# Hybrid-attention block on one core: value products of two heads on the two column halves, turned reciprocals, and three edits in the feed-forward part

## What is computed

```python
h = rms_norm(x, g_pre_mix) * (1.0 + sc1) + sh1
proj = h @ w_in            # 1220 columns: queries, keys, values, latents, indexer
# A: 8 heads, keys of the last 128 positions, a learned sink per head, ALiBi
# B: 8 heads, one shared key/value head; an indexer scores all visible keys,
#    each query keeps its 256 best; softmax over those, ALiBi
mix = concatenate([out_a, out_b]) @ w_o
x = x + gt1 * rms_norm(mix, g_post_mix)
h2 = rms_norm(x, g_pre_ffn) * (1.0 + sc2) + sh2
gate, up = split(h2 @ w_gate_up)
x = x + gt2 * rms_norm((silu(gate) * up) @ w_down, g_post_ffn)
```

## Time and profile before

| what | us |
|---|---|
| median of 3 runs | 3282.39 (3280.31 to 3283.53) |
| profiled execution, its own time | 3280.21 |
| its span, first to last instruction | 3278.4 |
| PE busy | 2893.9 (88%) |
| DVE busy | 1689.7 (52%) |
| ACT busy | 1569.7 (48%) |
| mean granted TensorE clock | 0.929 |

### The profile page before, as it was taken

The page is one execution under the profiler, slowest core; times in us unless marked ns, Lnnn a source line. Parts: engine busy times, 40 slices in busy tenths (PEclk is TensorE's granted clock), DMA queues, the critical chain, the costliest instruction groups (busy, mean ns, idle before and its releaser), DMA issues. The chain is left out here.

```text
span 3278.4 us, 42244 instructions
## 1 busy us (share of the span) xinstructions
PE 2893.9 (88%) x14392; PEld 2338.0 (71%) x14392; DVE 1689.7 (52%) x3088; ACT 1569.7 (48%) x3006; POOL 315.7 (10%) x989
## 2 busy tenths in 40 slices
PE   6678888787887888789898999999999999999997
PEld 2456666666676667678786887888877887888876
DVE  2246768586878868834454443254424443254422
ACT  0457787778777786875333222232223222232222
POOL 0112222212121120120111000000000000000000
PEclk8788888898988888889998999999999999999999
DMA  5000000000000010211465333343334333343323
GB/s 209 8 22 14 23 14 17 11 13 13 14 4 14 14 55 4 110 55 62 138 179 179 95 97 90 122 142 96 97 121 135 102 96 90 122 142 96 99 88 108
DMA packets 286884, 254.86 MB, mean 78 GB/s; under 512 B 8685, under 2 KB 238617, under 8 KB 286617
## 3 DMA queue, kind: packets, MB, share of 16 engines
q1 hardware_dynamic: 282584, 236.32, 23.3%
q10 hardware_dynamic: 4160, 16.78, 1.3%
HBM read 219.50 MB, written 33.57 MB: 77 GB/s over the span
## 5 line engine op out<-in xcount | busy, mean ns | idle before, releaser
L2002 ACT ACTIVATE p_hi<-raw 128x1024 fp32r<-128x1024 f32 x264 | 279.4, 1058 | 691.3 <-PE dbank L1972 352.4
L2079 DVE TENSOR_TENSOR p_lo<-raw,p_hi 128x1024 fp32r<-128x1024 f32 x264 | 323.4, 1225 | 429.6 <-ACT p_hi L2002 429.6
L1322 DVE TENSOR_SCALAR_CACHE_REDUCE above<-score,cand 128x384 uint8<-128x384 f32 (+6 forms) x224 | 315.8, 1410 | 4.3
L1172 ACT ACTIVATE signs<-score,pick 128x512 int8<-128x512 f32 (+6 forms) x224 | 304.4, 1359 | 28.1 <-POOL pick L684 19.7
L1150 ACT ACTIVATE logit<-tbank 128x512 f32<-128x512 f32 (+3 forms) x448 | 214.2, 487 | 209.0 <-PE tbank L903 205.8
L903 PE MATMUL tbank<-ident,logit 128*128 128x128 f32 x1336 | 249.5, 300 | 65.9 <-ACT logit L1140 57.0
L919 PE MATMUL obank<-vb,logit 128*128 128x64 f32 x2176 | 298.5, 282 | 0.0
L1970 PE MATMUL dbank<-p_hi,a_hi 128*128 128x512 f32 x704 | 277.8, 395 | 17.0 <-DVE a_lo L2106 13.8
L919 PEld LDWEIGHTS obank<-vb,logit 128*128 128x128 f32 x2176 | 292.1, 207 | 0.0
L1953 PE MATMUL gbank<-x_hi,p_hi 128*128 128x512 f32 x704 | 275.8, 392 | 14.8 <-DVE p_lo L2079 14.8
L788 PE MATMUL work<-w_in,h_T 128*128 128x512 f32 (+1 forms) x768 | 281.3, 514 | 0.7 <-ACT h_T L981 0.7
(11 more groups left out here) (216 smaller groups left out, 5115.6 us busy)
## 6 DMA issues: line engine op xcount, KB each, us to landing
raw<-in_w_gate_up SPq DMA_DIRECT2D x176, 512.0 KB, 3.8
raw<-in_w_down SPq DMA_DIRECT2D x88, 512.0 KB, 3.7
w_in<-in_w_ada ACTq DMA_DIRECT2D x4, 4096.0 KB, 13.3
wada<-in_w_ada SPq DMA_DIRECT2D x4, 2048.0 KB, 15.7
row<-in_x SPq DMA_DIRECT2D x16, 512.0 KB, 3.9
mixT<-oT SPq DMA_DIRECT2D x32, 256.0 KB, 2.3
x_rows<-in_x SPq DMA_DIRECT2D x16, 512.0 KB, 4.7
x<-x_rows SPq DMA_DIRECT2D x16, 512.0 KB, 3.1
```

Source lines behind the costliest of these rows:

```text
L1172: nc.scalar.activation(signs[:, 0:L], score[:, b % 2, 0:L], ACT.Sign, scale=-1.0, bias=pick[:].bitcast(F32), accum_out=less_more[:]).then_ ...
L1322: link(nc.vector.tensor_scalar(above[:, 0:L], score[:, b % 2, 0:L], cand[:].bitcast(F32), None, ALU.is_ge, ALU.add, accum_out=count[:]), b ...
L2002: nc.scalar.activation(p_hi[:, s], raw[:, s], ACT.Copy).then_inc(panel_high, 1)
L2079: nc.vector.tensor_tensor(p_lo[:, s], raw[:, s], p_hi[:, s].bitcast(F32), ALU.subtract).then_inc(panel_ready, 1)
```

## The change

**Value products.** The operands change places: v (128x64) is loaded, and 128 columns of transposed probabilities move. Two heads of a pair share v; head r of the pair writes partitions 64r to 64r+63 of `obank`, which comes out already turned. They are issued in turn: tile by tile, first one head, then the other. On PE the pair's groups stand in `head(i)` for even i (all but the last group, pair i-4) and behind the first piece of odd i (the last group, pair i-5).

**Rows.** Five rows of 1920 in a buffer of their own; the heads of the last B block use w_in's and the scores' place. w_o is loaded into the rows' place. DVE's first piece of head i now waits for the values of head i-5 and its pair.

**Totals.** `turn_output` and `copy_output` go. DVE inverts the totals two heads later and spreads them to 128x512 (`invert_totals`, one more DVE operation per output); PE turns those four tiles four heads later (`turn_totals`, in a slot of `tbank`), ACT copies them (`copy_totals`), and DVE multiplies `obank` by them one head later (`scale_output`).

**ffn.** The down part starts when all activation tiles but the last two are there, and waits for those before its 11th panel. The last panel of the last chunk goes tile by tile (`last_product`), with squares, roots (one column each) and the end (`last_tile`) by tile; half of the gains' product is made ahead (`gain_half`), and x1 of the last two tiles is loaded early into free places. The splitting of the next chunk's x is spread over the last four panels.

```diff
+RING = 5
+ROW = T - P
...
+        self.rows = ctx.enter_context(nc.sbuf_tensor("rows_of_logits", [P, RING * ROW], F32))
+        self.w_o = self.rows[:, 0:KD * D].rearrange("p (k n) -> p k n", n=D)
...
-            t += -(-len(key_tiles(kind, b)) // 4)
+            t += -(-len(key_tiles(kind, b)) // 4) + (h == 0 and len(self.group0) > 1)
...
+    def values_done(self, i):
+        pairs = self.heads[0:i // 2 * 2 + 1:2]
+        return sum(-(-len(key_tiles(kind, b)) // 4) for kind, b, _ in pairs)
+    def turned_totals(self, i):
+        return self.group0[i + 2] - 1 if i + 2 < len(self.group0) else self.group0[-1]
...
+        def row(i):
+            k = i % RING
+            if plan.heads[i][0:2] != ("B", NB - 1):
+                return shared.later.rows[:, k * ROW:(k + 1) * ROW]
+            return w_in_flat[:, k * T:(k + 1) * T] if k < 4 else score[:, 0, :]
...
-                sp.wait_ge(work_full, plan.work0["mod", MODS - 1] + 1)
+                sp.wait_ge(pv_done, plan.values_done(plan.head_no["B", NB - 2, HEADS - 1]))
                 for k in range(KD):
                     sp.dma_start(shared.later.w_o[:, k, :], w["w_o"][k * P:(k + 1) * P, :]).then_inc(shared.later.wo_in[k], 16)
...
+            def turn_totals(i):
+                kind, b, h = plan.heads[i]
+                t = plan.turned_totals(i)
+                pe.wait_ge(rtotal_ready, OUT_ORDER.index((kind, b)) + 1)
+                if t >= 2:
+                    pe.wait_ge(pt_ready, t - 1)
+                for j in range(4):
+                    mm = nc.tensor.transpose(tbank[t % 2][:, j * P:(j + 1) * P], rtotal_wide[:, j, :], ident[:])
+                mm.then_inc(pt_full, 1)
             def weighted_values(i, g):
...
+                pe.wait_ge(pt_ready, plan.group0[i + 1] + g + 1)
...
-                    pe.wait_ge(o_copied, o - 1)
+                    pe.wait_ge(o_made, o - 1)
                 for j, kt in enumerate(tiles):
-                    v = vb[:, kt, :] if kind == "B" else va[:, kt % 4, HD * (h // 4):HD * (h // 4 + 1)]
-                    mm = nc.tensor.matmul(obank[o % 2][:, h * HD:(h + 1) * HD], 
-                                          logit[:, i % 4, (4 * g + j) * P:(4 * g + j + 1) * P], v,
-                                          start=(g == 0 and j == 0), stop=(last and j == len(tiles) - 1))
+                    for r in range(2):
+                        v = vb[:, kt, :] if kind == "B" else va[:, kt % 4, HD * (h // 4):HD * (h // 4 + 1)]
+                        mm = nc.tensor.matmul(obank[o % 2][r * HD:(r + 1) * HD, h // 2 * P:(h // 2 + 1) * P], v,
+                                              row(i + r)[:, (4 * g + j) * P:(4 * g + j + 1) * P],
+                                              start=(g == 0 and j == 0), stop=(last and j == len(tiles) - 1))
                 mm.then_inc(pv_done, 1)
...
-                for c in range(max(pieces, groups, values)):
+                pair = i - 5 if i % 2 else i - 4
+                values = len(plan.groups(pair)) if 0 <= pair < n else 0
+                first = max(values - 1, 1)
+                for c in range(max(pieces, groups, values, 1)):
                     if c < pieces:
                         piece(i, c)
+                    if c == 0 and i % 2:
+                        for g in range(first, values):
+                            weighted_values(pair, g)
+                    if c == 0 and 4 <= i < n + 4 and plan.heads[i - 4][2] == HEADS - 1:
+                        turn_totals(i - 4)
                     if c < groups:
                         transpose_group(i - 2, c)
-                    if c < values:
-                        weighted_values(i - 3, c)
-                if 5 <= i < n + 5:
-                    turn_output(i - 5)
+                    if i % 2 == 0 and c < min(first, values):
+                        weighted_values(pair, c)
...
+            def copy_totals(i):
...
+                nc.scalar.activation(rtotal_T[:], pairs(tbank[t % 2][:]), ACT.Copy).then_inc(pt_ready, 1)
...
-                if c == 0 and i >= 4:
-
-                    dve.wait_ge(pv_done, plan.group0[i - 3])
+                if c == 0 and i >= RING:
+                    dve.wait_ge(pv_done, plan.values_done(i - RING))
...
+            def invert_totals(i):
...
+                dve.wait_ge(exp_done, i + 1)
+                sums = total[:, o % 2, :]
+                if kind == "A":
+                    link(nc.vector.tensor_tensor(sums, sums, exp_sink[:, o % 2, :], ALU.add))
+                link(nc.vector.reciprocal(rtotal[:], sums))
+                if o:
+                    dve.wait_ge(o_stored, 16 * o)
+                nc.vector.tensor_copy(rtotal_wide.rearrange("p j (r d) -> p (j r) d", d=HD),
+                                      rtotal[:].unsqueeze(2).to_broadcast([P, HEADS, HD])
+                                      ).then_inc(rtotal_ready, 1)
...
+                dve.wait_ge(pv_done, plan.values_done(i))
+                dve.wait_ge(pt_ready, plan.turned_totals(i) + 1)
+                nc.vector.tensor_tensor(oT[:], obank[o % 2][:].rearrange("p (j t) -> p j t", t=P), rtotal_T[:],
+                                        ALU.mult).then_inc(o_made, 1)
...
-                    elif i >= 4:
-                        scale_output(i - 4)
+                    else:
+                        if i >= 2:
+                            invert_totals(i - 2)
+                        if i >= 5:
+                            scale_output(i - 5)
...
+                if last:
+                    for t in range(2, TPC):
+                        sp.wait_ge(raw_given, c * PANELS + PANELS - TPC + t + 1)
+                        sp.dma_start(raw[:, t - 2], w["x1"][c * TOK + t * P:c * TOK + (t + 1) * P, :]
+                                     ).then_inc(x1_late[t - 2], 16)
...
+            for t in range(TPC):
+                c = NCHUNK - 1
+                step = 3 * c + 3 + 3 * t
+                root = rstd[:, t:t + 1]
+                pool.wait_ge(square_done, c * 2 * TPC + TPC + t + 1)
+                nc.gpsimd.tensor_tensor(root, ssq[:, 0, t:t + 1], ssq[:, 1, t:t + 1], ALU.add).then_inc(pool_step, 1)
...
+            def last_product(c, n, s, m):
+                pe.wait_ge(panel_ready, c * PANELS + UP + n + 1)
+                for t in range(TPC):
+                    for i in range(2):
+                        wh, wl = p_hi[:, s, i * HALF:(i + 1) * HALF], p_lo[:, s, i * HALF:(i + 1) * HALF]
+                        ah = a_hi[:, m * 2 + i, t * P:(t + 1) * P]
+                        al = a_lo[:, m * 2 + i, t * P:(t + 1) * P]
+                        nc.tensor.matmul(dbank[t][:], ah, wh, start=False, stop=False)
+                        nc.tensor.matmul(dbank[t][:], ah, wl, start=False, stop=False)
+                        mm = nc.tensor.matmul(dbank[t][:], al, wh, start=False, stop=(i == 1))
+                    mm.then_inc(tile_done, 1)
...
-                pe.wait_ge(act_ready, (c + 1) * KF + 2)
+                pe.wait_ge(act_ready, (c + 1) * KF)
...
+                    if n == DOWN - 1:
+                        pe.wait_ge(act_ready, (c + 1) * KF + 2)
+                    if last and n == 2 * DOWN - 1:
+                        last_product(c, n, n % 2, m)
+                    else:
+                        down_product(c, n, n % 2, m, m == 0, m == DOWN - 1, refill=(n == DOWN))
...
+            def gain_half():
+                dve.wait_ge(square_done, (NCHUNK - 1) * 2 * TPC + TPC)
+                for t in range(TPC):
+                    nc.vector.tensor_tensor(first_half[:, t, :], first_half[:, t, :], row[:, 0:HALF], ALU.mult
+                                            ).then_inc(half_gained, 1)
+            def last_tile(t):
+                c = NCHUNK - 1
+                to = out[:, t] if t < 2 else (th, act32)[t - 2][:].rearrange("p a n -> p (a n)")
+                x = x1[:, t] if t < 2 else raw[:, t - 2]
+                dve.wait_ge(root_done, c + t + 1)
+                if t < 2:
+                    dve.wait_ge(out_stored[t], c * (TPC // 2) * 16)
+                if t < 2:
+                    dve.wait_ge(x1_in[t], (c * (TPC // 2) + 1) * 16)
+                else:
+                    dve.wait_ge(x1_late[t - 2], 16)
+                dve.wait_ge(half_gained, t + 1)
+                nc.vector.scalar_tensor_tensor(to[:, HALF:], dbank[t][:], rstd[:, t:t + 1], row[:, HALF:],
+                                               ALU.mult, ALU.mult).then_inc(out_scaled, 1)
+                nc.vector.scalar_tensor_tensor(to[:, 0:HALF], first_half[:, t, :], rstd[:, t:t + 1], x[:, 0:HALF],
+                                               ALU.mult, ALU.add).then_inc(out_scaled, 1)
+                dve.wait_ge(out_scaled, 2 * (c * TPC + t) + 1)
+                nc.vector.tensor_tensor(to[:, HALF:], to[:, HALF:], x[:, HALF:], ALU.add).then_inc(out_made, 1)
...
+                for q in range(DOWN - 2, DOWN):
+                    for s in range(2):
+                        if not last:
```

(2 more changed lines are left out.)

## The result

| | before | after |
|---|---|---|
| median of 4 runs each | 3281.69 us (3280.31 to 3283.53) | 3259.56 us (3258.88 to 3263.82) |
| ratio | | 0.9935, 95% interval 0.9918 to 0.9952 |
| span of the profiled execution | 3278.4 us | 3257.2 us |
| first product of the output projection | 1575.99 us | 1587.15 us |
| from there to the end of the span | 1702.4 us | 1670.05 us |

The change makes the kernel 22 us faster; forecast were 64. The last two lines of the table split it: the feed-forward part became 32.4 us shorter (forecast 31.2), and everything before it 11.2 us **longer** (forecast 32.6 shorter). So one half of the prediction holds to about a microsecond, and the other has the wrong sign.

What follows compares the result with a forecast made beforehand. PE was taken to bound the feed-forward part, with mixing's limit changing from head to head. Mixing 32.6, down part's start 21.1 and end 10.1 sum to 63.8 us off 3280.2: forecast 3218, range 3188 to 3250.

Steps and rivals of the forecast that it cites:

- PE's relief, 78 us: Mixing: cheaper paired value products take 78 us of work from PE, 0.029 per old record.
- Price of sixteen records: Value products: four tiles of two heads cost 1.08 us in place of 1.62, the column halves overlapping.
- the slower rival: Value products: the halves run in turn, sixteen records cost 1.96 us, total 3294 us; chance 0.05.
- A stretches, 14 us: Mixing before 1406 us: two fifths of 58 us PE work lie in A stretches, 60% taken: 14 us gained.
- B stretches before 1406 us, 5: Mixing before 1406 us: three fifths of 58 us PE work lie in B stretches, 15% taken: 5 us gained.
- block 14, 5: B block 14: 8.6 us less PE work, but ACT is busy and PE partly idle: 5 us gained.
- The wait at the first piece of odd heads: Mixing: DVE waits there for the pair's last group, at most 1.1 us later; a new wait would show error.
- Block 15, 8.6, and the last heads, 2.0: End of mixing, PE busy throughout: block 15 gains 8.6 us, one head taking 6.1 instead of 7.2; last heads 2.0.
- The added vector operation: Mixing: one DVE operation of 128x512 per output, 0.69 us each, 22 us of DVE, charged with 2 us.
- Start of the down part, 21.1, and the end, 10.1: Feed-forward: no `a_lo` wait saves 13.8 us plus 7.3 of clock; finishing by tile saves 10.1 us.
- mixing is held by DVE and ACT: Rival: in mixing only block 15 and the last heads gain, total 3241 us; chance 0.20.
- w_o: Before the output projection: its 8 loads stay hidden; without cover up to 19 us would show.

Runs made afterwards that it cites:

- experiment 1: Feed-forward edits alone, mixing as in the kernel before the change: 3250.94 us, ratio 0.9911 against the kernel before.
- experiment 2: The changed kernel with all of a pair's value products in the even head, none behind the odd head's first piece: 3249.14 us, ratio 0.9905.
- experiment 8: The changed kernel without pairs: value products in the new form, one head at a time in every head: 3293.33 us, ratio 1.0040.
- experiment 9: The kernel of experiment 2 with the two heads' products one head after the other, not side by side: 3276.61 us, ratio 0.9994.
- experiment 5: The kernel of experiment 1 with every second key tile's value products left out: 3208.04 us, ratio 0.9776.
- experiment 13: The kernel of experiment 1 with five rows and all old-form value products of a pair in the even head: 3322.83 us, ratio 1.0122.
- experiment 11: The kernel of experiment 2 with a pair's groups before its last two moved into the odd head ahead: 3251.99 us, ratio 0.9915.
- experiment 3: The changed kernel with totals turned earlier on PE, at the end of the head three behind: 3269.44 us, ratio 0.9960.
- experiment 6: The kernel of experiment 2 with totals turned later, at the end of the head four behind: 3250.23 us, ratio 0.9902.

## Why the prediction was wrong

Against experiment 1 (3251), by the rates measured: PE's relief of 64 us (1130.5 to 1066.6) at 0.39 gives -25; the spread +5; the last group in the odd head +10 (experiment 2). That makes -10, and measured were +8.6. The 19 between them I put down to the order of the pairs. They are a remainder and not a run of their own, and as uncertain as the terms above are, they may be 12 to 28. Experiments 8 and 9 put the order at 23. The dearer the bunched products, the more the order costs: it is 19 us where sixteen records take 1.02 us, some 29 where they take 1.51 (3276.6 of experiment 9 against 3247 by the line through experiments 1 and 5 and the spread), and 72 with the old products of experiment 13. Experiment 11 spread the products in the late blocks and won nothing overall. So that the last group cost some 10 us is shown; that the rest is the order is argued.

By the steps of the prediction:

- **PE's relief, 78 us**: its busy time fell by 60 (1126.5 to 1066.6). The clock fell from 0.88 to 0.86 with it; at the old clock the same work would be about 24 us less, by estimate. Of the 78 the prediction let 34.6 reach the time, 0.44 for each, near the 0.39 that experiment 5 found. So the share wasn't the error.
- **Price of sixteen records**, forecast 1.08 us: measured 1.02, and 1.11 with the entering. Right, the reading of the 32-column products carried over, and the slower rival's mechanism (the halves in turn) falls. Its price was too high besides: 1.96 forecast, 1.51 measured in experiment 9.
- **A stretches, 14 us**: the step that failed most. They took 637.5 us before and 647.1 after, summed over all sixteen: 9.6 longer. It failed twice. The mean saving of 0.029 per old record was used for them, but their own runs are short. Two heads of block 10 that PE holds, before and after:

```profile
785.96 0.69 PE L888 MATMUL lbank<-ka,qa_hi 128*128 128x256 f32 x1
...
790.30 0.69 PE L888 MATMUL lbank<-ka,qa_hi 128*128 128x256 f32 x1
...
794.64 0.69 PE L888 MATMUL lbank<-ka,qa_hi 128*128 128x256 f32 x1
```

```profile
796.13 0.68 PE L907 MATMUL lbank<-ka,qa_hi 128*128 128x256 f32 x1
...
800.02 0.68 PE L907 MATMUL lbank<-ka,qa_hi 128*128 128x256 f32 x1
...
804.69 0.69 PE L907 MATMUL lbank<-ka,qa_hi 128*128 128x256 f32 x1
```

  8.68 us for two heads became 8.56: 0.12 saved, where the mean had given 0.23 for their eight old records. And the first three heads of an A stretch, which carry the large groups of the B heads before them, took 12.5 us more in sum (262.1 to 274.6): the even heads grew by 16.9 and the odd ones shrank by 4.4.
- **B stretches before 1406 us, 5**, and **block 14, 5**: block 14 gave 2.1 (88.1 to 86.0), the others together took 8.9 more (672.7 to 681.6). The wait at the first piece of odd heads was seen and put inside the 15% as nearly free; it cost 10 us in all.
- **Block 15, 8.6, and the last heads, 2.0**: the eight heads took 58.6 us and now 54.1, 6.8 for a head where 6.1 were forecast, and with the last heads, up to the first product of the output projection, 81.5 and now 76.5. So 5.0 came of 10.6. PE was busy there at every moment only as long as its work was evenly spread. Bunched, it waited about 1 us for ACT's copies at the start of every second head (the 1.09 us above). Experiment 11 has the forecast's saving there: 10.9 us against experiment 1.
- **The added vector operation**, 22 us of DVE charged with 2: it is 13.7, since a copy is quicker than the product that I took as its nearest row (427 against 691 ns), and it cost some 5, an estimate.
- **Start of the down part, 21.1, and the end, 10.1**: 21.2 and 11.2. Right, mechanism and size.
- **w_o**: PE's gap before its first product is 8.03 us, where 7.23 were in experiment 1. Hidden, as said.

So the 19 us forecast before 1406 us, less the 2 for the added operation, are the terms that failed: 17 us shorter were forecast and 18.5 longer measured. The rival "mixing is held by DVE and ACT" came nearest in its number (3241) and still isn't what happened: a microsecond off PE is worth 0.39 in the old order, and more in the new one. What failed was to count only PE's work. The prediction priced what the change removes and never priced that it moves most or all of a pair's products into one head of two.

## What to carry to other kernels

Where three engines hand work to each other in short steps and none is over 85% busy, the order of the work on the busiest can be worth as much as its amount, as it was here: put a price on the new order (which step now has double, which none) before counting the saving. Pairing work to make it cheaper bunches it; what spreading it over both steps gives back showed in the last block only (experiment 11), and the other work had been placed for the old order. A wait that grows in the trace needn't be a cost: ACT's for the totals was taken away in experiments 3 and 6, its wait for transposes rose by 32 and 23 us, and no time was won.

## What the runs showed of the chip

- Products on the two column halves overlap though both use all rows: sixteen records of 128 moving columns in 1.02 us, eight of one half alone in 1.02. Even in turn the seam overlaps: 1.51 for eight and eight.
- The granted clock followed PE's load in these runs, and so took back part of what PE was relieved of. Halving the products took the mixing's clock from 0.88 to 0.85, and the dearer products of experiment 8 raised it to 0.93. With the same products as before, bunching took it to 0.84 and added 56 us to PE's busy time.
